# Two transformer blocks on one core: first loads split, and norms, turns and projections between three stages interleaved by row groups

## The chip, the cores and the metric

The kernel runs on one NeuronCore of one Trainium2 chip. The metric is the device time of one execution in microseconds (us), lower being better; where several runs were timed it is their median. Everything is float32. Engines are named PE (TensorE, matmuls and transposes), DVE (VectorE), ACT (ScalarE), POOL (GpSimd) and SP (SyncE, which here only issues transfers).

## The reference, cut to what matters

A first block and then a second block are applied to x, 512 tokens of 1024 features. In the first block:

```python
h = rms_norm(x, attn_norm_g);  z = h @ w_in          # latents, differential q, k, v
x = x + concat(y_mla, y_diff) @ w_out
x = x + conv_ffn(rms_norm(x, ffn_norm_g), w_gate, w_up, conv_w, conv_b, w_down)
gate = sigmoid(rms_norm(x, ple_norm_g) @ w_ple_gate)
x = x + gate * (p @ w_ple_proj)
```

where `rms_norm(x, g) = x * rsqrt(mean(x*x) + 1e-6) * g`. The second block starts with a modulation and one wide projection, whose parts feed an attention with a learned choice of keys and a gated delta rule; a mixture of 32 experts follows.

```python
h = x * (1 + sc1) + sh1                              # sc1, sh1 from c and w_ada
q_att, c_kv, q_idx, k_idx, w_idx, qkv, a, b, z, gates = split(h @ w_in_2)
rel = relu(einsum('bqhd,bsd->bqhs', q_idx, k_idx))   # index scores, 8 heads
iscore = einsum('bqhs,bqh->bqs', rel, w_idx)         # causal; the best 128 keys are kept
g = -exp(a_log) * softplus(a + dt_bias)              # decay, summed inside chunks
```

## The kernel before, in words

**Tiling.** The 512 tokens lie in four row groups of 128, one token per partition: `x[:, q, :]` is group q. Products need features on partitions, so a group is "turned": eight 128x128 transposes on PE, four per PSUM bank, and DVE takes each bank out into `hT`, the turned copy, multiplying by the norm's gain on the way (`turned_in`, L1271 to L1281; with a shift it takes two passes). A float32 matmul is issued as two PE instructions in the trace, so the product of one group with a 512 column chunk of a 1024 row matrix is 16 PE instructions.

**Order.** Every engine runs a list in program order. Two rings of four PSUM banks join PE to DVE and to ACT; `bank` waits until the bank used four turns earlier was freed (`dve_free`, `act_free`), `full` signals that a bank is ready, and `take` on the reading engine follows in the same order. `taken` makes PE wait until everything is out of a ring. Weights come through three slots of SBUF: `items` lists them in order, and SP issues item n when item n-3 is recorded as done (`item_done`, L2285). The entry of `ple_proj` is recorded behind the last gate unit (`item_done[at_item]`), and `mixed`, three items later, is made of three loads: 256, 72 and 16 columns wide.

**Start.** SP loads x group by group, then all constants in one transfer (`cst`, of which the first 128 columns are the identity), then the column loads: 13 small transfers that bring gains, biases and convolution weights as rows into `staging`. PE waits for all of these, transposes `staging` in three pieces (L650), DVE copies them to `col`, and only then inverts the root of the variances, scales the groups into `xn` (two buffers, L1318) and takes the turned banks in. PE turns all four groups (`turn_x`), and then makes the latent products group by group (`by_token`). Then come the products for the relative biases (`biases`, L659), which wait for DVE's copy of the bias table (L1328) and for a second signal after ACT's exponentials. ACT's own list has the three activations L1955 to L1957 ahead of the copies of the latent rows (L1947).

**Feed-forward to gate stage.** The down projection is made in two column halves. In each one the four groups are accumulated over three slots of weights; in the last part (L893) the groups finish one after another. DVE adds each to x (L1520), and after the eighth it makes the sums of squares of all four groups (L1285), one root on ACT, and scales and turns the groups (L1291, L1278). Then PE turns p (the second input, 256 features) and DVE copies it. The gate stage is eight units of a gate product (1024 deep) and a projection of p (256 deep). ACT applies the sigmoid, DVE multiplies and adds to x (L1555, L1557).

**Gate stage to mixed.** PE waits for the last addition, turns all of x, DVE scales and shifts it in two passes per bank (L1280, L1281), and the mixed projection (344 columns: key latents, index keys and weights, decay inputs) follows by groups. A product for the index keys and four tiles for the index queries (`q_idx`) follow.

**Decay sums.** DVE and ACT normalise the key latents and make the decay gains through three table loads on ACT (L1570 to L1579, L2069 to L2072); PE waits, multiplies by a triangle (L944) and turns the key latents. Then eight products give the index scores of group 1, and the eight query tiles (`q_att`, two weight chunks of four tiles) alternate with the index scores of groups 2 and 3. DVE selects the keys of one group at a time: per head L1593 and L1596, then 16 rounds of L1599 and L1600. Attention starts on DVE behind the third selection.

Of the kernel before, what the change touches and what calls it, by code (L numbers as in the profile page):

```python
# [18 lines left out]
ALU = mybir.AluOpType  # L19
# [5 lines left out]
P = 128  # L25
SEQ, D = 512, 1024
# [133 lines left out]
def build(nc, t, out):  # L160
# [6 lines left out]
    with ExitStack() as ctx:  # L167
# [60 lines left out]
        eps_col, ln_eps_col = tiny(1), tiny(1)  # L228
        beta = tiny(NT * 8).rearrange("p (a b) -> p a b", a=NT)
# [47 lines left out]
        staging = place(ring + SLOTS * SLOT, 3, P)  # L277
# [92 lines left out]
        constants_loaded, columns_loaded = sem("constants_loaded"), sem("columns_loaded")  # L370
        x_loaded = [sem(f"x_loaded{q}") for q in range(NT)]
# [202 lines left out]
        def _(pe):  # L574
# [70 lines left out]
            pe.wait_ge(constants_loaded, 16)  # L645
            pe.wait_ge(columns_loaded, 16 * n_columns)
            for g in range(3):
                n = min(P, N_COLS - g * P)
                b = bank("dve")
                full(pe.transpose(b[:, 0:n], staging[0:n, g, :], ident[0:n, 0:n]), "dve")  # L650
# [231 lines left out]
            xnb = S2["xn"]  # L882
# [22 lines left out]
            turn_x(True)  # L905
            pe.wait_ge(p_loaded, 16)
            for q in range(NT):
                turn("dve", [S2["p"][:, q, k * P:(k + 1) * P] for k in range(2)])
            taken("dve")
# [3 lines left out]
            for c in range(2):  # L913
                w = weights("ple_gate")[0]
                for q in range(NT):
                    lq = slice(q * P, (q + 1) * P)
                    b = bank("act")
                    full(product(b[:, :], [(hT[:, k, lq], w[:, k, :]) for k in range(KD)]), "act")
                    b = bank("dve")
                    full(product(b[:, :], [(S2["pleT"][:, k, lq], wp[:, k, c * 512:(c + 1) * 512])  # L920
                                           for k in range(2)]), "dve")
                used("act")
            item_done[at_item] = (dve_full, done["dve"])

            taken("dve")
# [13 lines left out]
            used("act")  # L939

            to_wait(to_pe)
# [6 lines left out]
            taken("act")  # L948
# [7 lines left out]
            for c in range(2):  # L956
                by_feature("act", weights("q_att")[0], hT, 4)
                used("act")
                index_scores(2 + c)
# [262 lines left out]
        def _(dve):  # L1222
# [89 lines left out]
            for g in range(3):  # L1312
                n = min(P, N_COLS - g * P)
                V(dve.tensor_copy(col[:, g * P:g * P + n], take()[:, 0:n]), dve_free)
            invert(stat[:, 0:NT])
            for q in range(NT + 1):
                if q < NT:
                    V(ts(xn[:, q % 2, :], x[:, q, :], stat[:, q:q + 1], None, ALU.mult), tp_ready)  # L1318
                if q >= 1:
                    turned_in(q - 1, column("attn_norm_g"))  # L1320
# [223 lines left out]
            add_to_x()  # L1544

            norm_x(S2["xn"], flat(S2["conv"]), column("ple_norm_g"))
# [4 lines left out]
            for i in range(8):  # L1551
                c, q = divmod(i, NT)
                b = take()
                wait_next(sig_out)
                V(tt(S2["tmp"], b[:, :], S2["sig"][:, i % 2, :], ALU.mult), dve_free)  # L1555
# [4 lines left out]
            for q in range(NT):  # L1560
                turned_in(q, mod[:, 1, :], mod[:, 0, :])
            sm = S3["small"]
            for q in range(NT):
                V(dve.tensor_copy(sm[:, q, :], take()[:, 0:344]), dve_free)
# [794 lines left out]
```

## Time and profile before

| | |
|---|---|
| timed runs | 2607.34, 2604.69, 2606.67 us, median 2606.67 |
| the profiled execution | 2604.84 us, its span 2603.0 us |
| PE busy | 2288.9 us, 88% of the span |
| DVE busy | 1005.0 us, 39% |
| ACT busy | 450.5 us, 17% |
| POOL busy | 127.3 us, 5% |
| granted TensorE clock, mean | 0.95 of full speed |
| moved by DMA | 364.48 MB, mean 140 GB/s |

How to read it: times inside a profile count from the start of its span; the 1.8 us between span and execution lie outside the instructions. Busy PE includes matmuls at the lower clock. A line number is that of the instruction in the kernel; it can be that of a helper, as L611 (every product) and L630 (every turn).

### The profile page before, as it was taken

Reading aid. Unit: us, or ns where it says so; the run is one execution under the profiler, and the core shown is the slowest. Engines: PE = TensorE matmul, PEld = TensorE weight load, DVE = VectorE, ACT = ScalarE, POOL = GpSimd, SP = SyncE. Lnnn points to the kernel's source line nnn. Section 1 sums busy time; section 2 is a strip of 40 time slices with the busy share of each in tenths; the row PEclk is TensorE's granted clock in tenths of the full one; section 3 lists DMA queues with packets and bytes.
Section 4 is the critical chain, followed back from the end, with each engine's and each line's share of the span. In section 5 each row is a group of like instructions: output and inputs, shape, how many; then the busy total and the mean of one; then the engine's idle time right before and its main releaser. Section 6 shows DMA issues by size and latency. Waiting matters only on the chain.

```text
span 2603.0 us, 21118 instructions
## 1 busy us (share of the span) xinstructions
PE 2288.9 (88%) x7877; PEld 1140.8 (44%) x7877; DVE 1005.0 (39%) x1828; ACT 450.5 (17%) x840; POOL 127.3 (5%) x111
## 2 busy tenths in 40 slices
PE   5998778999999798897999877779999599999873
PEld 3444343444444344444444477764444333433331
DVE  2774552222200212486566657750003612222114
ACT  1125430000000010115232324430001100000002
POOL 0000000000000000000000032210000001101000
PEclk9999888999999999899999989999999699999997
DMA  6136403221122104110012000004123299999994
GB/s 219 59 128 211 162 1 73 74 88 65 58 96 72 65 0 151 34 63 33 33 65 92 6 1 1 1 9 171 65 85 157 93 412 426 426 426 427 426 425 199
DMA packets 97116, 364.48 MB, mean 140 GB/s; under 512 B 10372, under 2 KB 19121, under 8 KB 84465
## 3 DMA queue, kind: packets, MB, share of 16 engines
q1 hardware_dynamic: 86177, 340.61, 34.0%
q0 software_dynamic: 8720, 20.89, 2.1%
q10 hardware_dynamic: 2112, 1.57, 0.2%
q8 instruction: 65, 1.06, 0.2%
q14 instruction: 42, 0.34, 0.0%
HBM read 357.00 MB, written 17.57 MB: 144 GB/s over the span
## 4 chain that ended last, share of the span: by engine, by line
PE 72%; DVE 15%; DMA 6%; ACT 3%; issue 3%; SPq 0%; DVEq 0%; ACTq 0%; POOLq 0%
PE bank L611 47%; PE bank L1185 7%; PE bank L893 6%; PE bank L979 5%; PE bank L630 3%; DVE mem L1659 2%; DMA mem<-in_w_gate 2%; PE bank L773 2%; DMA mem<-in_w_down 2%; DMA mem<-in_w_up 1%; ACT mem L1947 1%; PE bank L669 1%; ACT L2087 1%; DMA mem<-in_conv_w 1%; DVE mem L1689 1%
## 5 line engine op out<-in xcount | busy, mean ns | idle before, releaser
L611 PE MATMUL bank<-mem 128*128 128x512 f32 (+7 forms) x3488 | 1450.3, 577 | 65.6 <-ACT mem L1947 19.1
L611 PEld LDWEIGHTS bank<-mem 128*128 128x128 f32 (+1 forms) x3488 | 648.6, 196 | 817.4 <-issue 744.1
L1185 PE MATMUL bank<-mem 128*64 128x512 f32 x1248 | 283.1, 609 | 32.0 <-DMA mem<-in_w_gate 11.2
L1947 ACT ACTIVATE mem<-bank 128x512 f32<-128x512 f32 (+5 forms) x291 | 161.5, 555 | 464.5 <-PE bank L630 167.5
L630 PE MATMUL bank<-mem 128*128 128x128 f32 (+1 forms) x820 | 139.6, 305 | 98.3 <-DVE mem L1418 24.4
L979 PE MATMUL bank<-mem 128*128 128x128 f32 x1280 | 165.6, 284 | 29.0 <-DVE mem L1690 26.4
L1185 PEld LDWEIGHTS bank<-mem 128*64 128x64 f32 x1248 | 95.3, 139 | 210.1 <-issue 196.8
L979 PEld LDWEIGHTS bank<-mem 128*128 128x128 f32 x1280 | 157.0, 199 | 34.6 <-DVE mem L1690 28.1
L630 PEld LDWEIGHTS bank<-mem 128*128 128x128 f32 (+1 forms) x820 | 103.8, 154 | 150.9 <-issue 41.2
L893 PE MATMUL bank<-mem 128*128 128x512 f32 x352 | 151.6, 592 | 0.9 <-DVE mem L1543 0.9
L1881 DVE TENSOR_TENSOR mem<-mem,bank 128x512 f32<-128x512 f32 x19 | 13.1, 690 | 286.6 <-PE bank L1185 203.9
L893 PEld LDWEIGHTS bank<-mem 128*128 128x128 f32 x352 | 66.5, 189 | 86.0 <-issue 84.3
L2210 POOL TENSOR_TENSOR mem<-mem 128x512 f32<-128x512 f32 x48 | 70.2, 1481 | 680.1 <-ACT mem L1947 612.5
L1530 DVE SCALAR_TENSOR_TENSOR mem<-bank,mem 128x511 f32<-128x511 f32 (+2 forms) x116 | 87.0, 750 | 4.1
L1889 DVE TENSOR_TENSOR mem<-bank,mem 128x512 f32<-128x512 f32 x38 | 26.3, 693 | 105.2 <-PE bank L1185 73.3
L1543 DVE TENSOR_TENSOR mem<-bank,mem 128x512 f32<-128x512 f32 x22 | 15.2, 693 | 124.8 <-PE bank L611 124.8
L1520 DVE TENSOR_TENSOR mem<-mem,bank 128x512 f32<-128x512 f32 x8 | 5.5, 690 | 147.0 <-PE bank L893 147.0
L1527 DVE TENSOR_SCALAR mem<-bank,mem 128x512 f32<-128x512 f32 x22 | 17.9, 812 | 110.2 <-PE bank L611 110.2
L2055 ACT ACTIVATE mem<-mem 128x512 f32<-128x512 f32 x22 | 13.9, 631 | 267.6 <-DVE mem L1530 267.6
L2163 ACT ACTIVATE mem<-bank 128x512 f32<-128x512 f32 x19 | 11.4, 599 | 275.9 <-PE bank L1185 204.7
L1659 DVE RECIPROCAL mem<-mem 128x512 f32<-128x512 f32 x16 | 53.7, 3354 | 3.5 <-ACT mem L2089 3.5
L1936 ACT ACT_TABLE_LOAD x10 | 12.8, 1283 | 235.7 <-DVE mem L1259 222.7
(290 smaller groups left out, 1338.0 us busy)
## 6 DMA issues: line engine op xcount, KB each, us to landing
mem<-in_w_gate SPq DMA_DIRECT2D x37, 2048.0 KB, 21.2
mem<-in_w_up SPq DMA_DIRECT2D x37, 2048.0 KB, 23.6
mem<-in_w_down SPq DMA_DIRECT2D x36, 2048.0 KB, 23.8
mem<-in_w_in SPq DMA_DIRECT2D x18, 2048.0 KB, 8.1
mem<-in_w_ada SPq DMA_DIRECT2D x12, 2048.0 KB, 7.9
mem<-in_w_out SPq DMA_DIRECT2D x4, 2048.0 KB, 10.4
mem<-in_w_ple_gate SPq DMA_DIRECT2D x2, 2048.0 KB, 8.0
mem<-in_w_br_att SPq DMA_DIRECT2D x2, 2048.0 KB, 7.9
```

Source lines behind the costliest of these rows:

```text
L611: last = pe.matmul(o, l, r, start=(i == 0), stop=(i == len(pairs) - 1))
L630: last = pe.transpose(b[0:width, i * P:(i + 1) * P], s, ident)
L669: last = pe.matmul(b[i:i + 32, :], cond_b[:, k, :], w[:, k, :], start=(k < 4), stop=(k >= 4))
L773: last = pe.matmul(o[:, k * P:SEQ], v_of(k, h), pT[:, h % nbuf, k, k * P:SEQ], start=(k == 0), stop=(k == NT - 1))
L893: last = pe.matmul(open_banks[q][:, :], S2["act"][:, k0 + k, q * P:(q + 1) * P], w[:, k, :], start=(i == 0 and k == 0), stop=(i == 2 and k ...
L979: last = pe.matmul(b[:, h * P:(h + 1) * P], lhs(h), rhs(h), start=True, stop=True)
L1185: last_ = pe.matmul(o[here, :], lhs[:, k, here], w[:, k, cols], start=(k == 0), stop=(k == kk - 1))
L1530: V(stt(o, b[:, 0:SEQ - back], w_col(taps_ - 1 - back), o, ALU.mult, ALU.add), signal if back == taps_ - 1 else None)
L1659: V(dve.reciprocal(sq, sq))
L1889: tt(yb[:, n % 2, at_], banks[5 + half][:, :], gate_rows[:, 1, at_], ALU.mult).then_inc(y_taken, 1)
L1947: C(act.activation(dst, src, ACT.Copy), act_free)
L2210: pool.tensor_tensor(delta[g][f"L{lv % 2}"], delta[g]["AT"], mask, ALU.mult)\
```

## The change

Five edits, in the order of the program. First, `ident` and the gain of the first norm are loaded on their own before the first weights; the rest of the constants and all column loads are issued between the first and the second item of weights. The first norm takes its gain from `first_gain`. The staging area moves and has a fourth plane. Second, the first turns alternate with the latent products; the column transposes (`columns`) come behind the latent products, and ACT waits for more `dve_free` before its three activations. Third, p is turned before the down projection, and the squares, roots, scalings and turns of the gate stage's norm are made per group, between the additions of the last down products and inside the gate stage. Fourth, the turns for the mixed projection are made per group, the first one inside the gate stage, the others around the wait for the mixed weights and between the mixed products. Fifth, the first two query tiles come ahead of the decay sums, the other two of the chunk behind the index scores of group 1, and the wait `taken("act")` becomes a wait for the index tiles only.

```diff
-        staging = place(ring + SLOTS * SLOT, 3, P)
+        staging = place(A0 + NT * LAT + 3 * 2048, 4, P)
...
+            pe.wait_ge(ident_loaded, 16)
+            pe.wait_ge(first_gain_loaded, 16)
+            full(pe.transpose(bank("dve")[:, 0:KD], staging[0:KD, 3, :], ident[0:KD, 0:KD]), "dve")
...
-            turn_x(True)
-            by_token("act", weights("lat")[0], hT, LAT)
+            def first_rows_turned(q):
+                to_wait(tp_ready)
+                for hf in range(2):
+                    turn("dve", [xn[:, q % 2, (4 * hf + k) * P:(4 * hf + k + 1) * P] for k in range(4)])
+                first_h[q] = done["dve"]
+            def latent_rows(q):
+                b = bank("act")
+                pe.wait_ge(dve_free, first_h[q])
+                full(product(b[:, 0:LAT], [(hT[:, k, q * P:(q + 1) * P], w_lat[:, k, :]) for k in range(KD)]), "act")
+            first_rows_turned(0)
+            first_rows_turned(1)
+            w_lat = weights("lat")[0]
+            latent_rows(0)
+            first_rows_turned(2)
+            latent_rows(1)
+            first_rows_turned(3)
+            latent_rows(2)
+            latent_rows(3)
             used("act")
+            columns()
             biases()
...
-            xnb = S2["xn"]
+            pe.wait_ge(p_loaded, 16)
+            for q in range(NT):
+                turn("dve", [S2["p"][:, q, k * P:(k + 1) * P] for k in range(2)])
             for c in range(2):
...
-            turn_x(True)
+            def x_rows_turned(q):
+                pe.wait_ge(sig_used, NT + q + 1)
+                rows_turned(x[:, q, :], q)
...
+            ple_rows_turned(0)
+            ple_rows_turned(1)
+            ple_rows_turned(2)
             wp = weights("ple_proj")[0]
             item_done.append(None)
             at_item = len(item_done) - 1
+            ple(0, 0)
+            ple(0, 1)
+            ple_rows_turned(3)
+            ple(0, 2)
+            ple(0, 3)
+            ple(1, 0)
+            ple(1, 1)
+            ple(1, 2)
+            x_rows_turned(0)
+            ple(1, 3)
             item_done[at_item] = (dve_full, done["dve"])
-            taken("dve")
-            pe.wait_ge(sig_used, 8)
-            turn_x(False)
-            w = weights("mixed")[0]
+            x_rows_turned(1)
+            weights("mixed")
             wmix = mixed
-            by_token("dve", wmix, hT, 344)
+            x_rows_turned(2)
+            mixed_rows(0)
+            x_rows_turned(3)
+            mixed_rows(1)
+            mixed_rows(2)
+            mixed_rows(3)
...
+            mark["index turned"] = done["act"]
+            q_att(0, 0)
+            q_att(0, 1)
             to_wait(to_pe)
...
-            taken("act")
+            pe.wait_ge(act_free, mark["index turned"])
             index_scores(1)
-            for c in range(2):
-                by_feature("act", weights("q_att")[0], hT, 4)
-                used("act")
-                index_scores(2 + c)
+            q_att(0, 2)
+            q_att(0, 3)
+            index_scores(2)
+            for m in range(4):
+                q_att(1, m)
+            index_scores(3)
```

`ple(c, q)` is one gate unit, `mixed_rows(q)` one group of the mixed product, both waiting for their group's turned rows (`h_ready`). DVE's list follows the same order:

```diff
-            for g in range(3):
-                n = min(P, N_COLS - g * P)
-                V(dve.tensor_copy(col[:, g * P:g * P + n], take()[:, 0:n]), dve_free)
+            V(dve.tensor_copy(first_gain, take()[:, 0:KD]), dve_free)
             invert(stat[:, 0:NT])
...
-            add_to_x()
-            norm_x(S2["xn"], flat(S2["conv"]), column("ple_norm_g"))
+            for q in range(NT):
+                down_added(0, q)
+            down_added(1, 0)
+            ple_squares(0)
+            down_added(1, 1)
+            ple_normal(0)
+            ple_squares(1)
+            down_added(1, 2)
+            ple_normal(1)
+            ple_squares(2)
+            down_added(1, 3)
+            ple_squares(3)
+            ple_turned(0)
+            ple_normal(2)
+            ple_turned(1)
+            ple_normal(3)
+            ple_turned(2)
...
+            ple_added(0, 1)
+            ple_turned(3)
...
+            ple_added(1, 2)
+            x_turned(0)
+            ple_added(1, 3)
+            x_turned(1)
+            x_turned(2)
+            mixed_taken(0)
+            x_turned(3)
```

ACT makes four small roots in place of one, and SP's list begins:

```diff
-            sp.dma_start(cst, t["shape_constants"]).then_inc(constants_loaded, 16)
-            for dst, src in column_loads:
-                sp.dma_start(dst, src).then_inc(columns_loaded, 16)
+            sp.dma_start(ident, t["shape_constants"][:, 0:P]).then_inc(ident_loaded, 16)
+            sp.dma_start(staging[0:KD, 3, :], column_loads[0][1]).then_inc(first_gain_loaded, 16)
             for n, (_, loads) in enumerate(items):
+                if n == 1:
+                    sp.dma_start(cst[:, P:], t["shape_constants"][:, P:]).then_inc(constants_loaded, 16)
+                    for dst, src in column_loads:
+                        sp.dma_start(dst, src).then_inc(columns_loaded, 16)
```

## Rows read from the trace of the kernel before

**Rows 1.** The page's chain that ended last: shares of the span by engine.

```profile
PE 72%; DVE 15%; DMA 6%; ACT 3%; issue 3%; SPq 0%; DVEq 0%; ACTq 0%; POOLq 0%
```

**Rows 2.** PE's waits: engine, line, releaser: us in total, times, longest.

```profile
PE bank L650 <- DMA mem<-in_conv_w: 23.4, 1, 23.4
...
PE bank L630 <- DVE mem L1291: 10.1, 3, 8.8
```

**Rows 3.** Timeline, first 70 us: start, length, engine, line, instruction [idle before <-releaser].

```profile
11.90 6.84 SPq L2285 DMA_DIRECT2D mem<-in_w_in  x2
...
14.29 0.21 ACT L1936 ACTIVATE mem<-mem 128x4 f32<-128x4 f32 x1
...
24.77 0.18 DVE L1256 RECIPROCAL mem<-mem 128x4 f32<-128x4 f32 x1
...
31.64 2.87 DVE L1278 TENSOR_TENSOR mem<-bank,mem 128x512 f32<-128x512 f32 x4
...
34.56 24.37 PE L611 MATMUL bank<-mem 128*128 128x416 f32 x64 [1.81 <-DVE mem L1278]
...
35.34 0.42 DVE L1328 COPY mem<-mem 32x512 f32<-32x512 f32 x1
...
38.46 0.21 ACT L1957 ACTIVATE mem<-mem 128x8 f32<-128x8 f32 x1
...
58.86 3.51 PE L659 MATMUL bank<-mem 32*128 32x512 f32 x11
...
66.00 15.42 PE L611 MATMUL bank<-mem 128*128 128x512 f32 x32 [1.28 <-DVE mem L1335]
```

**Rows 4.** DMA issues, first 120 us: KB each, median us to landing.

```profile
mem<-in_w_in SPq DMA_DIRECT2D x1, 1664.0 KB, 17.6
mem<-in_shape_constants SPq DMA_DIRECT2D x1, 1506.5 KB, 12.4
```

**Rows 5.** Timeline, feed-forward to gate stage.

```profile
890.00 0.69 DVE L1520 TENSOR_TENSOR mem<-mem,bank 128x512 f32<-128x512 f32 x1 [4.47 <-PE bank L893]
...
894.52 1.23 DVE L1285 CUSTOM_DVE_ANT_0 mem<-mem 128x1024 f32<-128x1024 f32 x1
...
899.88 0.69 DVE L1278 TENSOR_TENSOR mem<-bank,mem 128x512 f32<-128x512 f32 x1 [0.49 <-PE bank L630]
...
901.47 0.76 DVE L1291 TENSOR_SCALAR mem<-mem 128x1024 f32<-128x1024 f32 x1
...
909.84 15.45 PE L611 MATMUL bank<-mem 128*128 128x512 f32 x29 [1.31 <-DVE mem L1549]
```

**Rows 6.** Windows: busy per engine, then PE's granted clock, DMA share, GB/s.

```profile
909.80:912.00 2.20, 2.17 (x3) 1.13 (x4) 0.00 (x0) 0.00 (x0) 0.00 (x0) 0.50 0.00 0
```

**Rows 7.** Timeline, gate stage to mixed projection.

```profile
981.62 10.46 SPq L2285 DMA_DIRECT2D mem<-in_w_in  x5
...
985.42 0.66 PE L630 MATMUL bank<-mem 128*128 128x128 f32 x4 [0.27 <-DVE mem L1281]
...
995.60 8.85 PE L611 MATMUL bank<-mem 128*128 128x344 f32 x21 [5.16 <-DVE mem L1281]
```

**Rows 8.** DMA issues of the whole span: the narrowest part of the mixed weights.

```profile
mem<-in_w_in SPq DMA_DIRECT2D x1, 64.0 KB, 12.3
```

**Rows 9.** Timeline, decay sums and the first two selections.

```profile
1066.90 1.88 PE L944 MATMUL bank<-mem 128*128 128x8 f32 x8 [10.02 <-DVE mem L1579]
...
1073.09 1.01 DVE L1593 TENSOR_SCALAR mem<-bank,mem 128x256 f32<-128x256 f32 x2
...
1096.75 0.30 DVE L1601 TENSOR_SCALAR mem<-mem 128x256 f32<-128x256 f32 x1
...
1105.48 1.27 DVE L1593 TENSOR_SCALAR mem<-bank,mem 128x384 f32<-128x384 f32 x2 [8.43 <-PE bank L611]
...
1125.91 0.60 ACT L1947 ACTIVATE mem<-bank 128x512 f32<-128x512 f32 x1 [6.28 <-PE bank L611]
```

**Rows 10.** The chain in order of time, third selection: start, length, engine and line.

```profile
1141.54 0.75 DVE mem L1593
```

More of the change, by code:

```diff
@@ L903, in _, with rows_turned, ple_rows_turned, ple @@
                 used("dve")
-            turn_x(True)
-            pe.wait_ge(p_loaded, 16)
-            for q in range(NT):
-                turn("dve", [S2["p"][:, q, k * P:(k + 1) * P] for k in range(2)])
-            taken("dve")
+            h_ready = {}
+            def rows_turned(src, q):
+                for hf in range(2):
+                    turn("dve", [src[:, (4 * hf + k) * P:(4 * hf + k + 1) * P] for k in range(4)])
+                h_ready[q] = done["dve"]
+            def ple_rows_turned(q):
+                to_wait(tp_ready)
+                rows_turned(S2["xn"][:, q % 2, :], q)
+            def x_rows_turned(q):
+                pe.wait_ge(sig_used, NT + q + 1)
+                rows_turned(x[:, q, :], q)
+            ple_w = []
+            def ple(c, q):
+                if q == 0:
+                    ple_w.append(weights("ple_gate")[0])
+                lq = slice(q * P, (q + 1) * P)
+                b = bank("act")
+                if c == 0:
+                    pe.wait_ge(dve_free, h_ready[q])
+                full(product(b[:, :], [(hT[:, k, lq], ple_w[c][:, k, :]) for k in range(KD)]), "act")
+                b = bank("dve")
+                full(product(b[:, :], [(S2["pleT"][:, k, lq], wp[:, k, c * 512:(c + 1) * 512])
+                                       for k in range(2)]), "dve")
+                if q == NT - 1:
+                    used("act")
+            ple_rows_turned(0)
+            ple_rows_turned(1)
+            ple_rows_turned(2)
             wp = weights("ple_proj")[0]
@@ L939, in _, with q_att @@
             used("act")
+            mark["index turned"] = done["act"]
+            w_att = []
+            def q_att(c, m):
+                if m == 0:
+                    w_att.append(weights("q_att")[0])
+                b = bank("act")
+                full(product(b[:, :], [(w_att[c][:, k, m * P:(m + 1) * P], hT[:, k, :]) for k in range(KD)]), "act")
+                if m == 3:
+                    used("act")
+            q_att(0, 0)
+            q_att(0, 1)
             to_wait(to_pe)
@@ L1319, in _ @@
                 if q >= 1:
-                    turned_in(q - 1, column("attn_norm_g"))
+                    turned_in(q - 1, first_gain)
+            for g in range(3):
+                n = min(P, N_COLS - g * P)
+                V(dve.tensor_copy(col[:, g * P:g * P + n], take()[:, 0:n]), dve_free)
             dve.wait_ge(loaded, 16 * n_loads)
@@ L1550, in _, with down_added, ple_squares @@
                                   b[:, 0:256].rearrange("p (a b) -> p a b", a=2)), dve_free)
-            for i in range(8):
-                c, q = divmod(i, NT)
+            def down_added(c, q):
+                o = x[:, q, c * 512:(c + 1) * 512]
+                V(tt(o, o, take()[:, :], ALU.add), dve_free)
+            def ple_squares(q):
+                V(dve.tensor_tensor_reduce(flat(S2["conv"]), x[:, q, :], x[:, q, :], 1.0, 0.0, ALU.mult, ALU.add,
+                                           stat[:, q:q + 1]))
+                scale_var(stat[:, q:q + 1], D, EPS, var_ready)
@@ L2055, in _ @@
                 C(act.activation(S2["act"][:, m, :], S2["conv"][:, m % 2, :], ACT.Silu), silu_out)
-            root(stat[:, 0:NT])
+            for q in range(NT):
+                root(stat[:, q:q + 1])
             for i in range(8):
```

55 lines of the change are left out of this document (33 added, 22 removed).

## The prediction

> **What bounds the kernel now.** I read the chain of waits first. It shows a kernel bound by TensorE (PE): 72% of the span [rows 1], with VectorE (DVE) next. So what the change can give is PE idle time that ends on another engine or on a transfer. PE's list of waits names two long ones in the edited places: 23.4 us for the column loads at the very start, and the wait for the scaled rows of L1291 before the gate stage [rows 2]. The timelines of the four edited places give the rest: the start [rows 3], the seam between the feed-forward and the gate stage [rows 5], the seam between the gate stage and the mixed projection [rows 7], and the decay sums [rows 9]. The expert stage behind them waits for weight transfers, but these start only when routing is known, so what is won ahead of it is carried through to the end.
>
> **Start.** Before, the reciprocal comes at 24.77 behind three column copies, while ScalarE (ACT) had its root at 14.29+0.21=14.50 [rows 3]. With identity and gain ahead, DVE makes its first row group at about 14.6: 24.77-14.6 = 10.2 us earlier, if both loads land by then. The constants, 1506 KB, land 12.4 us after their issue at about 2.7, so at 15.1 [rows 4]; the 64 KB of them that are the identity come early in that stretch, an estimate of 12 to 13. The four groups took DVE from 24.77 to 31.64+2.87=34.51, so now they end at 24.3.
> The latent products no longer wait for all four. Their weights are the next term. Before, they were issued at 11.90 and landed 17.6 later, at 29.5, behind the constants [rows 3, 4]. Now the 1506 KB and the column loads stand behind them, and they follow x directly, with only identity and gain between. Bounds of the landing: 15.5 (1.7 MB behind x at the rate of the constants, 1506 KB in some 4 us) and 24 (an issue at 6.4 and the 17.6 kept). I take 18, near the constants' rate, since a shared engine also serves ACT's small loads. Group 0 is in hT at about 18.4 (14.6, a scaling of 0.76, eight transposes at the cold price of 0.66 per four or a little more, two passes of 0.69, and the second scaling between), and two groups' turns keep PE to about 19.3. From there: 24.4 for the 64 latent matmuls [rows 3] and 2.2 for two groups of turns between them (16 transposes: 0.66 per four is the cold price [rows 7], 0.55 my estimate while PE is dense): latent ends at 45.9, before at 58.9.
> Part of that is given back. The column transposes and copies (0.4+0.9), the lambda and gain work and the spread copy (34.51 to 35.34+0.42=35.76, 1.25) used to lie beside the latent products and now follow them. PE meets 2.6 us of it. The bias matmuls to the first dq product keep 66.00-58.86 = 7.1. The dq product starts at 45.9+2.6+7.1 = 55.6 to 55.8, before at 66.00 [rows 3]: **gain 10.2**. ACT now waits for the columns before it copies the latent rows out: it has about 3.3 us of activations (they ended at 38.46+0.21 before, behind a start near 35.4, [rows 3]) and four copies of 0.5, and ends 7.7 after the latent products, inside the 9.7. If that cover were gone it would cost about a microsecond. All bytes up to dq are the same, so dq lands as before, at about 35. POOL's queue is only moved with the bias rows. With the weights at 24 the gain is 5.5; at 15.5 it stays 10.2, as the turns end later.
>
> **Before down.** The four turns of p move ahead: eight transposes and the first DVE copy, 1.2 us on PE, not hidden, **-1.2** (an estimate from 0.66 per four cold transposes and a DVE pass; bounds half and twice of it).
>
> **Feed-forward to gate stage.** The last down product ends at 890.0 and the first gate product starts at 909.84: 19.8 us [rows 5]. Row groups 0, 1 and 2 of the second half finish 5.16 apart (4.47+0.69), so squares (1.23 and a read-out), root and scaling (0.76 and the reciprocal) of groups 0 and 1 and the squares of 2 are beside PE. After 890.0 DVE does the last add 0.7, squares 1.5 with the variance, then turned group 0 1.43, scaling 2 0.96, turned 1 1.43, scaling 3, turned 2. PE turns groups 0 and 1 meanwhile, group 2 from 894.6 to 895.8, and starts the gate product at 895.9: 13.9 us earlier. Groups 3 of this stage and 0 of the next are then turned inside the products, 2 x 1.1 on PE that used to be in the gaps: **+13.9-2.2**. What would be late next is the bank of turned group 1, freed by 896.0, which is met. Gate weights: the first chunk's slot is free long before, no wait. Nothing else queues on DVE that PE needs.
> Clock: the gate stage began at 0.50, the 1.2 GHz level, after the gap [rows 6], and was there until about 915.4, some 2.8 us lost. I count nothing of it back: the 2 to 6 us with short transposes remain. Bounds 0 and 2.8.
>
> **Gate stage to mixed.** This gap was 14.0 us, 981.6 to 995.60 [rows 7]. The text of the change makes it look removable (rows 0 and 1 turned early), but the mixed weights go into the slot of the projection weights and are issued only when the last gate unit is done: SP issues at 981.62, and the last of its three loads, 64 KB in 1024 rows of 64 B, lands 12.3 after its issue, two issues (0.7) later: 994.7 [rows 7, 8]. It was hidden with 0.9 us to spare. That does not move against the end of the stage. New: weights at +13.1, then the turns of group 2, which the program puts behind that wait, 1.3 (two fours of 0.66), then the first mixed product; group 3 is turned between products, 1.3: 15.7 against 14.0, **-1.7**. DVE's four passes per group (2.9 us) are now all hidden. Bounds: -3, and +11 if the load landed with the first load's speed.
> The Trainium skill speaks to this load: "DMA: Bandwidth & Descriptors", section "Specifications", puts the smallest piece for full rate at 512 B. The three loads' times of 5.3, 7.6 and 12.3 us for 1024, 288 and 64 KB agree: the smallest, with the shortest rows, is last, though it also queues behind the others. By the same page's "Rules for kernel authors" transfers under 64 KB are mostly overhead, which speaks against the split of the first loads; its table gives under 1 us for each, and as an estimate from it the latent weights would be 1.6 us later, without effect on the sum, as the turns end at 19.3.
>
> **Decay sums and query tiles.** PE waited 10.0 us until 1066.90 [rows 9]. Two query tiles of 6.88 (6.28+0.60 between ACT's copies) now fill it, from 1057.0 to 1070.7. They are no extra work, but they push the decay sums, and with them DVE's selections: first selection work came 6.2 after the decay sums began (1073.09), now it begins at about 1076.5, 3.4 later, and a selection lasts 24.0 (to 1096.75+0.30). So it ends at 1100.5, while PE has finished tiles 2 and 3 by 1094.3 and four index products by 1097. The other four need banks that DVE frees only after 1100.5, at 1.25 per head: PE stands 4 us, and creeps for 4. Then four tiles with the last index product, 28.4, to 1133.5, and DVE starts the third selection at 1134.4. Before: the second selection waited 8.43 on DVE at 1105.48 and the third started at 1140.8 (0.75 before 1141.54) [rows 9, 10]. The stage ends with that selection, about 36 us of DVE, then attention. Gain 6.4; a longer cold stretch of the clock takes up to 2: I take **+6**. Bounds 3 and 10.
>
> **Sum.** 10.2-1.2+13.9-2.2-1.7+6 = 25.0 us. The profiled execution took 2604.84 (span 2603.0, the rest lies around it); 2579.8. The median shown is 2606.67, 1.8 above the profiled one, so I predict 2581.5.
>
> **Rivals.**
> A, the latent weights are late: the small loads on ACT's queue and the issue limit of SP keep the latent weights at 24 to 29.5. For: SP's own issues were blocked for 6.84 us at 11.90, and the landing took 17.6. Against: the constants just before flowed freely. Gain of the start 5 to 0: total 15 to 20, 2587 to 2592. Chance 0.14.
> B, the clock is kept: gate stage, latent products and the query tiles start at 2.4 GHz; 2.8, and 1 to 3 elsewhere: total 30, 2576. The page "TensorE: Matmul & The Clock Gate" (the Trainium skill), "What's actually happening", says that activity releases a throttle that is otherwise on; by that it depends on how dense the new turns are. Chance 0.12.
> C, the mixed weights are not what ends the seam: the small load is quick when it is alone. Then the first mixed product starts 3 after the stage: total 36, 2570. Against: x is written out beside it just as before. Chance 0.06.
> D, no change, gaps only shift: the third selection and the weights absorb all. It needs both of the large terms (start, gate seam) to fail; chance 0.03.
> E, slower: in the gate stage the inserted turns and their bank waits keep PE at the 1.2 GHz level. At 0.43 per matmul its 160 matmuls would take 69 us more at half speed; from 36% of that lost (25 us) it is slower, fully it gives 2651. Against: the level came back within 6 us of dense products before [rows 6]. Chance 0.03.
> My forecast has 0.62. Within 0.2% (5 us), which is what a measurement tells from no change: 0.03 from D and 0.01 from the foot of A. Faster 0.92, slower 0.04 (E and what I can't name). The range takes in A's upper part and B: 2573 to 2592.
>
> **What would show it.** The first row group's scaling on DVE at 14 to 16 us; the first dq product at 55 to 57; first gate product 6 us behind the last down product; a PE wait of 11 to 12 us for in_w_in before the turns of group 2 in the mixed seam; a PE wait of about 4 us for the selection's work behind query tile 3. It is wrong if the mixed wait is absent, or if the latent products start after 22.

## The result and the profile after

The changed kernel takes 2580.36 us (median of four runs, 2577.90 to 2580.43), the kernel before 2606.15: a ratio of 0.9895 as estimated from all runs (the medians alone give 0.9901), 95% interval 0.9878 to 0.9911. By the medians that is 25.8 us faster, forecast were 25.0. The profiled execution took 2577.90 with a span of 2576.0, 27.0 less than before. The chain of waits keeps its shape, its first line answers to [rows 1]:

```profile
PE 73%; DVE 15%; DMA 6%; ACT 3%; issue 3%; SPq 0%; DVEq 0%; ACTq 0%; POOLq 0%
```

Read as landmarks, the two profiles say where the time went. Each row is the start of one instruction in both traces (the end, for the latents); the last column is what the steps of the prediction add up to at that point. "dq" is the product that makes the differential queries, the first one behind the products for the relative biases (the bias stage); a "seam" is the stretch between two stages; "cold" is said of PE at the lower of its two clock levels, 0.50 granted.

| landmark | before | after | earlier by | forecast |
|---|---|---|---|---|
| latent products end | 58.9 | 42.4 | 16.5 | 13.0 |
| first dq product | 66.00 | 54.74 | 11.3 | 10.2 |
| first down product | 738.26 | 729.53 | 8.7 | 9.0 |
| first gate product | 909.84 | 887.65 | 22.2 | 22.9 |
| mixed weights issued (gate stage done) | 981.62 | 960.45 | 21.2 | 20.7 |
| index key product | 1016.92 | 995.54 | 21.4 | 19.0 |
| first selection | 1073.09 | 1054.38 | 18.7 | 15.6 |
| third selection | 1140.74 | 1114.02 | 26.7 | 25.4 |
| end of span | 2603.0 | 2576.0 | 27.0 | 25.0 |

The timeline of the start, against [rows 3] (start, length, engine, line, instruction, idle before and its releaser):

```profile
11.46 0.24 PE L649 MATMUL bank<-mem 8*128 8x8 f32 x1 [11.46 <-DMA mem<-in_attn_norm_g]
...
12.70 0.18 DVE L1341 RECIPROCAL mem<-mem 128x4 f32<-128x4 f32 x1 [0.63 <-ACT mem L2072]
...
18.14 5.87 PE L613 MATMUL bank<-mem 128*128 128x416 f32 x16 [0.74 <-DMA mem<-in_w_in]
...
42.41 0.54 PE L658 MATMUL bank<-mem 128*128 128x128 f32 x3
...
44.96 8.51 PE L667 MATMUL bank<-mem 32*128 32x512 f32 x16 [2.02 <-issue]
...
54.74 16.11 PE L613 MATMUL bank<-mem 128*128 128x512 f32 x32 [1.27 <-DVE mem L1421]
```

The wait for the gain ends at 11.5, the weights land 14.2 us after their issue at 3.94, at 18.1, and a bias stage that took 7.1 takes 9.8. The row of the transfer, against [rows 4]:

```profile
mem<-in_w_in SPq DMA_DIRECT2D x1, 1664.0 KB, 14.2
```

The timeline of the two seams, against [rows 5, 7]. Between the last down product (DVE takes it at 881.2, before the change at 890.0) and the first gate product there are 6.4 us in place of 19.8, and before the mixed product PE waits 11.68 us for weights, where it had waited for DVE:

```profile
880.97 1.91 PE L632 MATMUL bank<-mem 128*128 128x128 f32 x16
...
885.89 1.97 PE L632 MATMUL bank<-mem 128*128 128x128 f32 x8 [3.01 <-DVE mem L1646]
...
887.65 19.44 PE L613 MATMUL bank<-mem 128*128 128x512 f32 x40
...
960.45 9.37 SPq L2425 DMA_DIRECT2D mem<-in_w_in  x5
...
972.97 1.97 PE L632 MATMUL bank<-mem 128*128 128x128 f32 x8 [11.68 <-DMA mem<-in_w_in]
```

And the decay sums with the selections, against [rows 9, 10]. The second selection follows the first without a pause, the third still waits 5.19 us for PE:

```profile
1049.11 0.95 PE L1026 MATMUL bank<-mem 128*128 128x8 f32 x8
...
1054.38 1.01 DVE L1729 TENSOR_SCALAR mem<-bank,mem 128x256 f32<-128x256 f32 x2
...
1078.40 1.27 DVE L1729 TENSOR_SCALAR mem<-bank,mem 128x384 f32<-128x384 f32 x2
...
1114.02 1.54 DVE L1729 TENSOR_SCALAR mem<-bank,mem 128x512 f32<-128x512 f32 x2 [5.19 <-PE bank L613]
```

### The profile page after: what moved, and what is told of

Read it like the earlier page. It is cut to its first block, busy times and chain, and to the rows that moved or that the text cites. A ratio compares the mean times of both kernels' runs of the same rounds, so it can differ in the third digit from the quotient of the medians.

```text
span 2576.0 us, 21148 instructions
## 1 busy us (share of the span) xinstructions
PE 2282.1 (89%) x7878; PEld 1139.6 (44%) x7878; DVE 1006.5 (39%) x1835; ACT 450.7 (17%) x843; POOL 127.4 (5%) x111
## 4 chain that ended last, share of the span: by engine, by line
PE 73%; DVE 15%; DMA 6%; ACT 3%; issue 3%; SPq 0%; DVEq 0%; ACTq 0%; POOLq 0%
PE bank L613 46%; PE bank L1270 7%; PE bank L924 6%; PE bank L1064 5%; PE bank L632 3%; DVE mem L1795 2%; DMA mem<-in_w_gate 2%; PE bank L802 2%; DMA mem<-in_w_down 2%; DMA mem<-in_w_up 2%; DMA mem<-in_w_in 1%; ACT mem L2083 1%; PE bank L677 1%; DVE mem L1736 1%; DVE mem L1735 1%
## 5 line engine op out<-in xcount | busy, mean ns | idle before, releaser
L1270 PE MATMUL bank<-mem 128*64 128x512 f32 x1248 | 277.5, 599 | 39.3 <-DMA mem<-in_w_up 15.1
L2017 DVE TENSOR_TENSOR mem<-mem,bank 128x512 f32<-128x512 f32 x19 | 13.1, 691 | 285.0 <-PE bank L1270 203.9
L2191 ACT ACTIVATE mem<-mem 128x512 f32<-128x512 f32 x22 | 13.9, 631 | 267.6 <-DVE mem L1616 267.6
L2300 ACT ACTIVATE mem<-bank 128x512 f32<-128x512 f32 x19 | 11.4, 598 | 272.6 <-PE bank L1270 201.3
```

Of the source, the lines that this page charges most:

```text
L1270: last_ = pe.matmul(o[here, :], lhs[:, k, here], w[:, k, cols], start=(k == 0), stop=(k == kk - 1))
```

## The experiments

All are edits of the changed kernel; times are medians of four or five runs, ratios are estimated from all runs and are to the kernel before on the same chip. Code is cut, and in part told in words. An interval is some 4 us to either side, so kernels less than that apart are judged by landmarks of their profiles.

**The same kernel again.** No edit.

> The changed kernel once more, unchanged, beside the same kernel before. Theory (identical stretches differ between executions by where the granted clock falls, 2 to 5 us in all): 2580.4, 2577 to 2583, with a profile whose stretches before and behind the edited places differ from the first one's by up to 4 us. Rival (stretches of one program repeat within 0.5 us, and the differences of the last four kernels are effects of their edits): every landmark within 0.5 us of the first profile.

2579.51, ratio 0.9902 (0.9887 to 0.9917). Its start and both seams repeat within 0.4 us (dq at 55.00, first mixed product at 974.76), and so did the long stretch from the projections to the feed-forward; only the end of the span moved by more, 0.9. That speaks for the rival at first sight. But the same stretch, with the same instructions, differs between the kernels of this study. The windows of it (busy of PE, PEld, DVE, ACT, POOL, then PE's granted clock) for the changed kernel, for the one with the gate seam put back, and for the one with the mixed seam put back, whose programs are equal up to here:

```profile
93.90:378.00 284.10, 242.20 (x985) 123.33 (x985) 172.49 (x451) 108.68 (x252) 2.23 (x4) 0.90 0.35 123
```

```profile
95.10:383.10 288.00, 246.19 (x986) 124.71 (x985) 172.32 (x451) 108.74 (x252) 2.23 (x4) 0.89 0.34 121
```

```profile
94.40:375.70 281.30, 238.72 (x985) 122.08 (x985) 172.37 (x451) 108.74 (x252) 2.23 (x4) 0.92 0.35 124
```

281.3 to 288.0 us for one list of instructions: PE's busy time and clock carry the difference, DVE's does not move. So several us of a span belong to where the lower clock falls, and no edit can be credited with them. Both theories were half right: a repeat can agree to 0.5 us over most of its length, and equal instructions in two kernels can be 6.7 us apart. Single executions of one kernel differ too: nine of the kernel before, on the chip of this run, took 2603.02 to 2616.09.

**The start put back.**

```diff
-            sp.dma_start(ident, ...); sp.dma_start(staging[0:KD, 3, :], ...)
+            sp.dma_start(cst, ...); all column loads
-            turns and latent rows interleaved; columns() behind them
+            columns() first; all turns; taken("dve"); all latent rows
```

> The changed kernel with its start put back (constants and all column loads ahead of the first weights, all turns ahead of the latent products, column copies first). Theory (the start is worth what the first dq product moved, and everything behind it moves along): the dq product returns from 54.7 to about 66, so 2580.4 + 11.3 = 2591.7, 2590 to 2594. Rival (transfers behind the start hide part, so that it is given back before the expert stage): under 4, 2584 or less.

2589.31, ratio 0.9937 (0.9924 to 0.9951), 8.9 us over 2580.4. The first dq product starts at 63.79, 9.05 later than in the changed kernel, and 8.1 of it are still there at the down products and 7.9 at the first selection: hardly anything is given back. The rival falls. The size is below 11.3 since here the latents took 22.67 us for 64 matmuls where the kernel before took 24.37 [rows 3]: it did not meet the lower clock.

**Which part of the start: loads.**

```diff
+            constants and column loads issued here, ahead of items
             for n, (_, loads) in enumerate(items):
-                if n == 1: (constants and column loads)
```

> The changed kernel with the constants and column loads ahead of the first weights again, identity and first gain still first, row groups as changed. Theory (the order of the loads is most of the start's gain): weights land near 29 in place of 18, the first dq product at 65 to 66, 11 later, 2591. Rival (the early first norm is most of it): under 4 later, 2584.

2592.01, ratio 0.9943 (0.9930 to 0.9957), 11.7 us slower by the medians and 15.5 between the profiled executions. The timeline of it: the latents wait for their weights until 29.95, about as long as before the change (29.5).

```profile
29.95 8.71 PE L613 MATMUL bank<-mem 128*128 128x416 f32 x16 [10.90 <-DMA mem<-in_w_in]
```

The dq product starts at 69.75, 15.0 later, where the theory had 11: the weights are 11.8 later, and the latents take 27.1 us in place of 24.3, with a granted clock of 0.50 in their first 3 us. That is even 3.8 behind the kernel before: with serial column work behind late weights, the other half of the edit costs.

**Which part of the start: row groups.**

```diff
-            first_rows_turned(0); first_rows_turned(1); latent_rows(0); ... interleaved
+            first_rows_turned(0..3); latent_rows(0..3)
```

> The changed kernel with all four groups turned ahead of the latent products, the loads as changed. Theory (the weights are there at 18.1, so the products now wait for DVE's last turned group at about 22.5, and two groups' turns leave their middle): latents end 2.5 later, 2583, 2581 to 2585. Rival (the row groups are what moved the start): 6 to 8 later, 2587.

2576.79, ratio 0.9884 (0.9869 to 0.9899): not slower, which neither expected. The latents start at 21.62 and end at 44.03, 1.6 later. But the bias stage behind them took less, and the dq product starts 0.2 earlier than with row groups. The timeline of that stage:

```profile
46.58 6.69 PE L667 MATMUL bank<-mem 32*128 32x512 f32 x16 [2.01 <-issue]
```

Its windows show the clock at 0.65 in this stage against 0.52 for the changed kernel (below). The later landmarks agree to 0.2 us with those of the changed kernel (first down product, at 729.62 against 729.53), and its dq product, at 54.54, is no later than in any of the seven profiles that share the changed kernel's start, the two of the changed kernel and the five of kernels edited only behind it (54.6 to 55.4). So interleaving turns and latents moves dq by nothing here: what it wins at the latents, the bias stage gives back. What moved the start is that the weights come early. The early first norm alone gave nothing, as the run with the weights behind the constants shows; early weights with a late norm were not run, and in the kernel before the turned rows end at 34.5 [rows 3], so the gain is put down to both together.

**What the start gave back.**

```diff
             latent_rows(2)
+            columns()
             latent_rows(3)
             used("act")
-            columns()
```

> The changed kernel with the column transposes between the latent products of groups 2 and 3, so that the copies, the lambda work and ACT's three activations lie beside the last latent product. Theory (the part given back at the start is a serial 2.6 us and a bias stage at the lower clock, 9.8 in place of 7.1): the first dq product 4.6 us earlier, at 50.1; 2576. Rival (the bias stage keeps its 9.8 us, only the serial part goes): 52.7, 2578.4.

2574.71, ratio 0.9880 (0.9864 to 0.9895). The dq product starts at 50.13, the 50.1 of the theory, and the rival, 52.7, falls. That it fits to the tenth is luck: the latents started 1.0 later here (19.12), and the bias stage took 6.1 us, not the 7.1 that the theory gave it. From the first latent product to the dq product it is 31.0 us (31.3 in the kernel with both mends, below); in the seven profiles that share the changed kernel's start it is 36.3 to 36.6. So the mend is worth some 5 us. The windows of the bias stage, of the changed kernel and of this one (here with 1.1 us of latents ahead of it):

```profile
45.00:55.00 10.00, 8.72 (x17) 4.38 (x18) 4.64 (x12) 4.77 (x9) 0.52 (x1) 0.52 0.49 187
```

```profile
42.90:50.10 7.20, 5.75 (x20) 2.83 (x18) 4.40 (x10) 2.31 (x6) 0.24 (x1) 0.93 0.69 230
```

The fall of the clock does not need the pause, though: it came in this stage, 16 matmuls that the DVE copies pace, with the pause and without. Windows around the fall and the return, first of the changed kernel (the stage begins at 44.96), then of this one (it begins at 44.05):

```profile
45.00:47.00 2.00, 2.00 (x5) 1.11 (x6) 0.25 (x1) 1.94 (x4) 0.00 (x0) 0.58 1.03 401
57.00:59.00 2.00, 2.00 (x3) 0.67 (x2) 1.90 (x4) 0.00 (x0) 0.00 (x0) 0.50 0.84 348
```

```profile
49.00:51.00 2.00, 0.87 (x1) 0.50 (x2) 1.76 (x8) 0.00 (x0) 0.70 (x1) 0.53 1.05 394
55.00:57.00 2.00, 2.00 (x5) 0.74 (x4) 0.28 (x3) 1.49 (x2) 0.00 (x0) 0.76 0.00 0
```

Behind 2.0 us of pause the clock was at its 1.2 GHz level from the start of the stage until 59, some 14 us (1.00 from 59 to 61). With PE busy up to the stage it was at that level from about 49 to 56, some 7 us, and most of that under the dq product. The kernel before, with no pause either, shows the fall in the same place (0.50 at the start of dq, 66 to 68). How much the pause costs varied: the bias stage behind it took 7.4 to 9.8 us in those seven profiles, with the low level lasting 10 to 14 us.

**The gate seam put back.**

```diff
-            ple_squares / ple_normal per group between the down additions
+            all additions, all squares, one root; then scale and turn
-            ple_rows_turned(0..2) ahead, (3) inside the gate stage; p ahead of down
+            ple_rows_turned(0..3), p turned here, taken("dve")
```

> The changed kernel with only the feed-forward to gate stage seam put back (norm after the last addition for all groups, turns of all four, p turned there). Theory: the seam grows from 6.5 to 20 us (+13.5), but the p turns before the down products (1.1), one group's turns inside the gate stage (1.0) go, and the cold stretch grows by about 1: +12.4, 2592.8, 2591 to 2595. Rival (the clock is most of it, the gap little): the seam in the trace differs by under 8 us and the rest lies inside the gate stage's products.

2595.46, ratio 0.9951 (0.9937 to 0.9964), 15.1 slower, just above the range of the theory. Of the 18.9 by which its profiled span is longer, 5.2 were there before the feed-forward, 3.9 of them in the stretch shown above. From the first feed-forward product to the index key product it loses 10.9: the seam 12.9, less 1.1 for p and 1.0 in the mixed seam and its products, which were not edited. The gate stage itself took 72.9 us against 72.8: one group's turns left it, and it began with more cold products. So up to its end the edit cost 11.9, near the theory's 12.4, and the clock was not most of it; the rest of the 15.1 lies outside the edited places. In its chain of waits the gate stage, one unbroken run of PE, begins at 904.62, where the changed kernel has it at 887.65:

```profile
904.62 63.44 PE bank L613 x140
```

**The mixed seam put back.**

```diff
-            x_rows_turned(0) inside the gate stage; (1) | weights | (2) mixed(0) (3) ...
+            pe.wait_ge(sig_used, 8); x_rows_turned(0..3); taken("dve"); mixed_rows(0..3)
```

> The changed kernel with only the gate stage to mixed projection seam put back (all four groups turned after the last addition). Theory (the narrow load of the mixed weights ends the seam in both orders): no slower, about 0.8 faster since one group's turns leave the gate stage, 2579.6, 2578 to 2582; the seam is about 14 us, ended by DVE. Rival (the turns by groups did shorten this seam, and something else paid for it): 8 to 12 slower, 2588 to 2592.

2578.22, ratio 0.9892 (0.9876 to 0.9908). No slower, as the theory has it. Mixed weights are issued at 957.29 and the first mixed product follows 13.96 later, in the timeline released by DVE:

```profile
971.25 9.01 PE L613 MATMUL bank<-mem 128*128 128x344 f32 x24 [5.16 <-DVE mem L1364]
```

From the first gate product to the index key product it is 1.4 us shorter than the changed kernel. So the fourth edit, taken alone, is worth nothing.

**The wait it ran into, taken away.** The weights go to memory that the feed-forward has left, and are issued behind the second gate weights.

```diff
-        mixed = slot_view(n, KD, 344)
+        mixed = place(A0 + 14208, KD, 344)
...
+            pe.wait_ge(mixed_loaded, 48)
...
+                if n == mixed_item - 1:
+                    for dst, src in mixed_loads:
+                        sp.dma_start(dst, src).then_inc(mixed_loaded, 16)
```

> The changed kernel with the mixed weights in memory of their own (the place of the dead feed-forward activations), issued behind the second gate weights, some 80 us before their use. Theory (the narrow load alone holds the seam): no PE wait for in_w_in there, first mixed product some 3 us behind the gate stage in place of 14.5, and no cold stretch: 11 to 13 faster, 2568. Rival (DVE's two passes per group end the seam next): 6 to 8 faster, 2573.

2568.25, ratio 0.9856 (0.9841 to 0.9871): 12.1 under the changed kernel. Its timeline and its clock in the 5 us of the first mixed products:

```profile
958.36 1.91 PE L635 MATMUL bank<-mem 128*128 128x128 f32 x16
...
961.54 4.91 PE L616 MATMUL bank<-mem 128*128 128x344 f32 x16 [1.28 <-DVE mem L1370]
```

```profile
960.00:965.00 5.00, 3.72 (x15) 2.38 (x14) 4.76 (x8) 0.00 (x0) 0.78 (x1) 1.00 0.97 299
```

The narrow load held the seam: 3.0 us from the end of the last gate product to the first mixed one in place of 14.3, and no cold stretch. Only now can the fourth edit be worth something: in the old order of turns DVE ended the seam, 14.0 behind the stage, in the run above, and early weights would not have moved that. This is argued; early weights with the old order were not run.

**No tile ahead.**

```diff
-            q_att(0, 0); q_att(0, 1); to_wait(to_pe)
+            to_wait(to_pe)
```

> The changed kernel with no query tile ahead of the decay sums, four between index scores 1 and 2, four between 2 and 3, as before. Theory (the stage ends with DVE's third selection, which the two tiles ahead move by 5.3): 2580.4 + 5.3 = 2585.7, 2584 to 2588. Rival (the whole PE wait of 10.0 us was the gain): 2590.4.

2592.63, ratio 0.9948 (0.9934 to 0.9962): 12.3 slower, more than either theory. DVE's timeline:

```profile
1086.13 1.27 DVE L1731 TENSOR_SCALAR mem<-bank,mem 128x384 f32<-128x384 f32 x2 [10.53 <-PE bank L613]
...
1122.97 1.54 DVE L1731 TENSOR_SCALAR mem<-bank,mem 128x512 f32<-128x512 f32 x2 [6.42 <-PE bank L613]
```

The selections wait 10.5 and 6.4 us for PE, in the kernel before 8.4 [rows 9] and 4.8 with the same order:

```profile
1140.74 1.54 DVE L1593 TENSOR_SCALAR mem<-bank,mem 128x512 f32<-128x512 f32 x2 [4.83 <-PE bank L611]
```

The windows of the first 20 us of that work, first this kernel, then the kernel before:

```profile
1050.00:1070.00 20.00, 19.66 (x46) 10.07 (x47) 18.55 (x53) 0.60 (x1) 0.00 (x0) 0.77 0.00 1
```

```profile
1071.00:1091.00 20.00, 19.21 (x49) 9.96 (x50) 18.54 (x52) 0.73 (x2) 0.00 (x0) 0.88 0.00 1
```

0.77 against 0.88 is 2.2 us of PE in the first 20. At the second selection's start it is 0.71 against 0.81 over 9 us, and 0.97 against 1.00 over the 28 behind it: as an estimate 3.9 us in all. By landmarks the third selection starts 9.0 later than in the changed kernel; 5.3 of that is what the changed kernel gained here over the kernel before, and the clock accounts for the other 3.7. In the profiles another 3.5 us lie behind the third selection, in code that was not edited. That the fifth edit also makes the stage less open to a low clock (its second selection has no pause to lose) is not shown; in the changed kernel the same first 20 us ran at 0.76.

**Another share of tiles.**

```diff
-            q_att(0, 0); q_att(0, 1) | 2 behind scores 1 | 4 behind scores 2
+            q_att(0, 0) | 3 | 3 | 1 behind scores 3
```

> The changed kernel with one query tile ahead of the decay sums, three behind index scores 1, three behind 2, one behind 3. Theory (DVE's 91 us of selections set this stage; they start 2.7 earlier and starve less): third selection ends 4 us earlier, 2576.5. Rival (PE with the last tile and the 27.7 us of key and value products becomes last): no gain, 2580.

2581.09, ratio 0.9907 (0.9892 to 0.9920). DVE did what the theory says: the third selection starts at 1114.72 with no wait and its last instruction starts 110.8 us behind the last index query tile, against 115.0. But the rival ends the stage: PE is in the key and value products until 1158.0 (its timeline),

```profile
1129.52 28.50 PE L613 MATMUL bank<-mem 128*128 128x512 f32 x66
```

and the first value product of the attention comes 126.1 behind the index queries in place of 122.5. Two ahead is the better share by this landmark, by 3.6 us; the medians, 0.7 apart, do not tell the two. Both engines end nearly together there.

**Both mends.** `columns_early` and `mixed_own_home` in one kernel.

> The changed kernel with both mends: the column transposes between the latent products of groups 2 and 3, and the mixed weights in memory of their own. Theory (two separate places, both on the path): the gains add, 4.7 + 11.7 = 16.4 off 2580, 2563.6, 2560 to 2567. Rival (what is won earlier is given back at the index scores): 2568, no better than the second mend alone.

2566.09 (2562.70 to 2572.68), ratio 0.9851 (0.9836 to 0.9866), the fastest of all by its median; in its profile the dq product starts at 49.68 and the first mixed product 3.0 behind the gate stage. Its profiled span, 2560.8, is 3.0 under that of the second mend alone, not the 4.6 by which the first mend alone brings the dq product forward: the stretch shown above took 2.7 more here (284.2 against 281.5). The 3.0 us by which it leads at the first down product are still there at the third selection (1097.78 against 1100.77), so the rival, a loss at the index scores, falls by the landmarks. The gains hold at their places, and the median lies in the theory's range; that the medians add is not shown, at 2.2 us between this one and the second mend alone and such intervals.

## Why the prediction was right, step by step

**Start, 10.2 against 11.3.** The sum was near by two errors against each other. The first scaling comes 12.1 earlier, not 10.2: I held the end of ACT's root at 14.5, but it ended at 12.6, since ACT's list of loads ended 1.9 earlier. Weights were at 18.1, forecast 18. The latents ran at 2.4 GHz from the start, 24.3 us with the turns against 26.6; the 24.37 that I took from [rows 3] held some cold products (0.50 from 35 to 38). The 2.6 us that I let PE meet behind the latents were 2.55, but the bias stage did not keep its 7.1: it took 9.8 at a granted clock of 0.52. So the latents ended 3.5 us ahead of the forecast, the bias stage gave 2.7 back, and that 10.2 was near is luck in part. That the row groups count for the start was wrong: turns first gives the same dq start. Rival A is refuted by the landing.

**Before down, -1.2 against -1.1** (728.42 to 729.53). Right. The other 1.4 us between dq and down lie in stretches that were not edited: the dq product took 16.11 us against 15.42 [rows 3], cold until 59 behind the bias stage, and the long stretch above 284.1 against 283.4.

**Feed-forward to gate stage, 13.9 against 13.5.** The last additions, squares and turns ran as forecast; the turns of group 2 took 1.8 before the gate product could start, not 1.2. The price was misread: the 0.66 for four turns, which I called the cold price, was taken at the full clock. The windows of those four turns in the kernel before, and of the eight of group 2 in the changed kernel:

```profile
985.42:986.10 0.68, 0.65 (x4) 0.41 (x4) 0.67 (x1) 0.00 (x0) 0.00 (x0) 1.00 1.09 349
```

```profile
885.89:887.65 1.76, 1.76 (x8) 1.76 (x9) 1.66 (x4) 0.00 (x0) 0.00 (x0) 0.50 1.06 404
```

Nothing of the cold stretch was to come back, and about 1.0 did: the gate stage took 72.8 us with 2.1 of turns in it, against 71.8. The windows of the gate stage's start, against [rows 6], show the level back by 892, 4 us in, and not after 5.6:

```profile
887.00:889.00 2.00, 2.00 (x7) 1.33 (x6) 1.90 (x4) 0.00 (x0) 0.00 (x0) 0.50 0.58 214
889.00:891.00 2.00, 2.00 (x3) 0.67 (x2) 0.70 (x2) 0.00 (x0) 0.00 (x0) 0.50 0.00 0
891.00:893.00 2.00, 2.00 (x5) 0.91 (x4) 0.00 (x0) 0.00 (x0) 0.00 (x0) 0.79 0.00 0
```

Rival B was thus right in part: the latents and the query tiles ahead of the decay sums (1.00 from 1044 to 1050) did start at 2.4 GHz, the gate stage did not and gained only by a shorter cold stretch, and in the bias stage the change lost the clock. Its page, "TensorE: Matmul & The Clock Gate" of the Trainium skill, section "What's actually happening", has activity release the throttle; the windows of the bias stage agree in direction, 0.52 where PE had paused and 0.93 where it had not, though the clock fell without a pause too, later.

**Gate stage to mixed, -1.7 against +0.2.** The mechanism was the forecast one: the weights landed 12.5 behind their issue (13.1), PE waited 11.68 for them (11 to 12), and the first mixed product came 14.3 behind the stage (14.4), where it had been 14.0. The mis-sized term is the turns. Those of group 2, behind the wait, took 1.8 and not 1.3, but they ran in the cold stretch that the mixed products had paid for before: with group 3's turns in them, for which I had added 1.3, the mixed products took 20.7 us, against 21.3 without. Rival C, the load quick by itself, falls: it took 11.4 us (12.3 in [rows 8]). The page "DMA: Bandwidth & Descriptors" of the Trainium skill, "Specifications", puts the smallest piece for full rate at 512 B; the load's 64 B rows lie under it, and the runs show only that an early issue hides the load's time, not what share of it is due to the rows.

**Decay sums, +6 against +5.3.** Selections began 2.7 later (3.4), the second had no pause, the third waited 5.19. PE's stall behind tile 3 was at most 3.1 us, I had 4. That the fifth edit is what gained it stands on the run with no tile ahead, which loses it again, 5.3 by the order and 3.7 by the clock.

**The size.** 25.0 against 25.8 in the medians and 27.0 in the profiles. By the landmarks the edited places gained more than forecast, 11.3 - 1.1 + 13.5 - 1.0 + 0.2 + 5.3 = 28.2, and stretches that were not edited lost 1.2 of it. So the mechanisms were right and the sum was 3.2 too small: it had the start 1.1, the gate stage with its inserted turns 1.2 and the mixed seam with its products 1.9 too low, the gate seam 0.4 and the last step 0.7 too high. That the medians lie within 0.8 of the forecast is luck in part. The four put-backs cost 8.9, 15.1, -2.1 and 12.3 by the medians, which adds up to 34; by the landmarks of their own places they cost 8.1, 10.9, -1.4 and 9.0, which is 26.6, near the 26.7 that the change had gained by the third selection.

Two of the signs came a little outside what I wrote, the first scaling at 12.91 (14 to 16) and the dq product at 54.74 (55 to 57); the others came as written, and neither sign of being wrong did. I had written the range for unknown waits; the stretches of equal instructions show that 2 to 7 us of it belong to something that no step of a sum can hold. Rivals D and E did not occur.

## What to carry to other kernels

Before work is moved up to a seam, look for the load that the seam's next product needs and at what event its buffer is released: here that one wait, at first hidden behind DVE with 0.9 us to spare by my estimate, made a whole rearrangement worthless, and 11 KB per partition of dead memory gave it back. When serial work is moved from beside a matmul to behind it, its price is not only its length: the stage after it can run cold for longer, and here 2 us of pause ahead of a sparse stage cost some 5 us. And judge an edit by the landmarks of its own stage; the total carries several us of clock that other stages drew.

## What the runs showed of the hardware beyond that

Equal instruction lists took 281.3, 284.1 and 288.0 us in different kernels, in steps rather than spread: those with the mixed seam put back, with the weights in their own place and with the early columns had 281.3 to 281.5, those with the gate seam put back and with the other share of tiles 288.0, the others, the kernel before among them, 283.4 to 284.2. What chooses the step is open. The same kernel run again had 284.10 both times, but the instructions ahead do not choose it: seven of these profiles share them too, and took 281.3, 281.4, 283.7, 284.1, 284.1, 288.0 and 288.0. One repeat does not exclude chance. A transfer's landing depended on its place in the queue: behind x, the 1664 KB of latent weights landed at 18.1 behind 64 KB and 4 KB, and at 29.9 behind the constants and 13 small column loads.
